# An S5 state-space step inside a streaming encoder: 32-wide TensorE tiles, three slabs in each step, tokens in natural order

## The reference, cut to what matters

```
z = h @ w_in;  u, q, k, v, g_s, g_a = split(z)
# 64 groups of 16 channels, 64 complex states each
bu[l] = Bbar[g] @ u[l, g]                      # 16 channels -> 64 complex states
s[l]  = Abar * s[l-1] + bu[l]                  # over the tokens (prompt from 0, sample from the given state)
y[l]  = Re(C[g] @ s[l]);  y = gelu(y + ssm_d * u);  y = y * sigmoid(y @ w_glu)
```

## Time and profile before

| | us |
|---|---|
| median of 3 runs | 1407.69 |
| lowest, highest | 1404.42, 1412.64 |
| the profiled execution | 1413.75 |
| its span | 1411.8 |
| mean granted TensorE clock in it | 0.946 of full speed |

### The profile page before, as it was taken

One profiled execution on the slowest core, in us unless ns is written; L12 is line 12 of the kernel. 1 busy time (PEld: TensorE's weight loads), 2 busy tenths in 40 slices (PEclk: granted clock), 3 DMA queues, 4 the chain that ended last, 5 costly groups with the idle time before them and its releaser, 6 DMA issues.

```text
span 1411.8 us, 22570 instructions
## 1 busy us (share of the span) xinstructions
PE 1279.8 (91%) x9314; PEld 1247.9 (88%) x9314; DVE 717.4 (51%) x1022; ACT 529.5 (38%) x960; POOL 309.6 (22%) x276
## 2 busy tenths in 40 slices
PE   3999899996849899999987989988999999999996
PEld 3999888996748799999987988988999999999995
DVE  5344888888786543454466333235432433433433
ACT  6446434443325562333544223224312312312322
POOL 1069988888100000000211000024000000000020
PEclk9999999998768989999999999888999999999996
DMA  6142112221100053332344420220232232332311
GB/s 177 58 146 65 56 49 90 94 94 47 40 14 1 7 186 109 107 115 76 113 157 131 146 60 1 60 61 24 81 99 65 81 100 60 90 88 70 94 30 67
DMA packets 183410, 113.29 MB, mean 80 GB/s; under 512 B 6976, under 2 KB 175872, under 8 KB 183008
## 3 DMA queue, kind: packets, MB, share of 16 engines
q1 hardware_dynamic: 178400, 104.56, 24.9%
q10 hardware_dynamic: 4928, 7.56, 1.5%
HBM read 100.11 MB, written 12.12 MB: 79 GB/s over the span
## 4 chain that ended last, share of the span: by engine, by line
PE 72%; DVE 16%; ACT 6%; issue 4%; DMA 2%; POOL 0%; SPq 0%; DVEq 0%; ACTq 0%; POOLq 0%
PE gp L1546 29%; PE gp L1923 29%; DVE z L1283 3%; ACT ub L757 3%; PE sp L1784 2%; PE sp L1898 2%; DVE wL L1044 1%; PE gp L1875 1%; DVE rot L1262 1%; PE sp L1664 1%; PE gp L1683 1%; PE sp L1652 1%; DVE rot L1264 1%; DVE x L1123 1%; DVE raw L1103 1%
## 5 line engine op out<-in xcount | busy, mean ns | idle before, releaser
L1044 DVE TENSOR_TENSOR wL<-wraw,wH 128x1024 fp32r<-128x1024 f32 x164 | 216.3, 1319 | 138.5 <-ACT wH L615 138.1
L615 ACT ACTIVATE wH<-wraw 128x1024 fp32r<-128x1024 f32 x164 | 172.8, 1054 | 241.0 <-PE gp L1923 121.4
L1546 PE MATMUL gp<-aH,wH 128*128 128x288 f32 (+1 forms) x1088 | 241.9, 305 | 10.9 <-DVE aL L1079 4.0
L590 POOL TENSOR_TENSOR acc<-acc,sq 128x576 f32<-128x576 f32 x28 | 41.8, 1492 | 924.8 <-ACT sq L667 924.8
L1546 PE MATMUL gp<-aL,wH 128*128 128x288 f32 (+1 forms) x1088 | 237.8, 301 | 0.0
L1546 PE MATMUL gp<-aH,wL 128*128 128x288 f32 (+1 forms) x1088 | 237.6, 301 | 0.0
L1546 PEld LDWEIGHTS gp<-aH,wH 128*128 128x128 f32 x1088 | 181.4, 195 | 13.6 <-issue 11.8
L1546 PEld LDWEIGHTS gp<-aL,wH 128*128 128x128 f32 x1088 | 181.3, 194 | 0.0
L1546 PEld LDWEIGHTS gp<-aH,wL 128*128 128x128 f32 x1088 | 180.8, 194 | 0.0
L1923 PE MATMUL gp<-aH,wH 128*128 128x288 f32 x512 | 112.0, 301 | 9.1 <-DVE aL L1110 4.5
L1923 PE MATMUL gp<-aH,wL 128*128 128x288 f32 x512 | 110.8, 298 | 0.0
(11 more groups left out here) (298 smaller groups left out, 2215.4 us busy)
## 6 DMA issues: line engine op xcount, KB each, us to landing
wraw<-in_w_ff SPq DMA_DIRECT2D x64, 512.0 KB, 4.1
wraw<-in_w_in SPq DMA_DIRECT2D x36, 512.0 KB, 3.8
gates_scratch<-sq ACTq DMA_DIRECT2D x16, 288.0 KB, 2.2
gate<-gates_scratch SPq DMA_DIRECT2D x16, 288.0 KB, 4.5
wraw<-in_p_att SPq DMA_DIRECT2D x8, 512.0 KB, 4.3
wraw<-in_w_glu SPq DMA_DIRECT2D x8, 512.0 KB, 4.3
wraw<-in_p_ssm SPq DMA_DIRECT2D x8, 512.0 KB, 4.2
wraw<-in_w_out SPq DMA_DIRECT2D x8, 512.0 KB, 4.2
```

The lines of the kernel that those rows point to most:

```text
L590: g.tensor_tensor(acc[:], acc[:], sq[:, k % 2], ALU.add).then_inc(sq_used, 1)
L615: s_.activation(wH[s][:], wraw[w][:], ACT.Copy).then_inc(wh_done, 1)
L1044: v.tensor_tensor(wL[s][:], wraw[w][:], wH[s][:], ALU.subtract).then_inc(wl_done, 1)
L1546: last = mm(gp[:, b + h, 0:n], w[:, k, :], y[:, k, c0:c0 + n], start=(k == 0 and w is wH[s] and y is xh), stop=(k == KT - 1 and w is wL[s]))
```

## The change

- `SSM_SLABS` has three slabs for each of eight steps (12 to 35). TensorE's step m is now: slab, outputs(m-1), slab, table(m+1), slab, inputs(m+1); outputs(7) stays in the tail.
- ub and `u_build` are gone. TensorE reads u from z directly, with a step of four tokens (`by_time`), and writes y into PSUM with one bank for each of the four tokens of a block.
- `table`: the Toeplitz table is built as four column tiles of 32, with 64 columns each; toep shrinks to 128x128, and ScalarE copies it, in one operation.
- `inputs`: 32 matmuls on row tiles of 32 rows (pair j on rows 32j, PSUM bank j), four accumulated for each.
- `outputs`: 32 matmuls on column tiles of 32 and 40 on 32x32 tiles at (32j, 32j).
- `y_out` is one operation of 128x576 and sits inside `scan_and_turn` of the next step.
- `e_table` keeps one multiplication on GpSimd; er comes from a third sine on ScalarE, rho from four scaled copies on ScalarE, and the factor 2 of ei moves into VectorE's operations. zm gets a third buffer.
- ScalarE's copy of the final states and the eight stores move behind `soften(0)`; the transposes for it move behind band_scores(1) and y_out(7), and band_step(0) waits for the copy.

```diff
-SSM_SLABS = {m: list(range(12 + 4 * m, 16 + 4 * m)) for m in range(-1, 5)}
-SSM_SLABS[5], SSM_SLABS[6] = [32, 33], [34, 35]
+SSM_SLABS = {m: list(range(12 + 3 * m, 15 + 3 * m)) for m in range(8)}
...
+        Y0, T0 = 2 * NB, 3 * NB
+        v_slot = [sp_[:, :, c * NB:(c + 1) * NB] for c in range(2)]
+        y_slot = sp_[:, :, Y0:Y0 + NB]
+
+        def by_time(ap):
+            return ap.rearrange("p (c s) -> p s c", s=SB)
...
-                if m >= 2:
-                    pool.wait_ge(y_ps, m - 1)
-                zb = zm[m % 2]
+                if m >= 3:
+                    pool.wait_ge(y_ps, m - 2)
+                zb = zm[m % 3]
...
-                g.tensor_tensor(eim[:], e0, e1, ALU.mult)
-                seq(g.tensor_tensor(erm[:], e0, e0, ALU.mult))
-                g.tensor_scalar(eim[:], eim[:], 2.0, 0.0, ALU.mult, ALU.add)
-                g.tensor_scalar(erm[:], erm[:], -2.0, 1.0, ALU.mult, ALU.add)
-                g.tensor_tensor(rho[m % 2][:], bk(thl[:, 2, ds(PB * m, PB)], [P, PB, NB]),
-                                cmask[:].unsqueeze(1).broadcast_to([P, PB, NB]), ALU.mult).then_inc(e_ready, 1)
+                g.tensor_tensor(ei[m % 2][:], e0, e1, ALU.mult).then_inc(e_ready, 1)
...
+                if m >= 2:
+                    act.wait_ge(h_ready, m - 1)
+                for j in range(PB):
+                    s_.activation(rho[m % 2][:, j, :], cmask[:], ACT.Copy, scale=thl[:, 2, PB * m + j:PB * m + j + 1])
                 seq(s_.activation(earg[:, 1], earg[:, 0], ACT.Abs))
+                s_.activation(er[m % 2][:].rearrange("p j c -> p (j c)"), earg[:, 1], ACT.Sin, scale=-TWO_PI, bias=halfpi[:, 0:1])
...
-                for j in range(PB):
-                    src = z[32 * j:32 * j + 32, ds(m, 1), :].rearrange("p o (c s) -> p (o s) c", s=SB)
-                    for s in range(SB):
-                        last = s_.activation(ub[b][32 * s:32 * s + 32, j, :], src[:, s], ACT.Copy)
-                last.then_inc(u_built, 1)
...
+                if m >= 2:
+                    act.wait_ge(y_ps, m - 1)
+                s_.activation(toep[m % 2][:].rearrange("p (b c) -> p b c", b=2), sp_[:, 0:2, T0:T0 + 64], ACT.Copy).then_inc(toep_cp, 1)
...
             def y_out(m):
                 dve.wait_ge(y_ps, m + 1)
-                for j in range(PB):
-                    r = slice(32 * j, 32 * j + 32)
-                    zu = z[r, ds(m, 1), :].rearrange("p o (c s) -> p (o s) c", s=SB)
-                    for s in range(SB):
-                        last = v.scalar_tensor_tensor(zu[:, s], zu[:, s], gains[r, ds(8 * G_D + m, 1)],
-                                                      sp_[32 * s:32 * s + 32, j // 2, (j % 2) * NB:(j % 2 + 1) * NB],
-                                                      ALU.mult, ALU.add)
-                last.then_inc(y_evac, 1)
+                u = by_time(z[:, m, :])
+                v.scalar_tensor_tensor(u, u, gains[:, 8 * G_D + m:8 * G_D + m + 1], y_slot, ALU.mult, ALU.add).then_inc(y_evac, 1)
...
+            def ssm_step(m):
+
+                t0 = SSM_SLABS[m][0] + AHEAD
+                turn_in(m)
+                split_l(t0, t0)
+                scan_and_turn(m)
+                split_l(t0 + 1, t0 + 1)
+                split_l(t0 + 2, t0 + 2)
...
+                    pe.wait_ge(v_read, m)
+                    pe.wait_ge(toep_cp, m)
+                    pe.wait_ge(y_evac, m)
...
+                for h in range(2):
                     for c in range(2):
-                        last = mm(sp_[0:32, 2, j * P:(j + 1) * P], xm[:, c, j, SB - 1, :],
-                                  zm[b][:, c, j, 0:SB, :].rearrange("p s k -> p (s k)"), start=(c == 0), stop=(c == 1))
+                        for j in range(PB):
+                            last = mm(sp_[32 * j:32 * j + 32, h, T0:T0 + 64], xm[:, c, SB - 1, j, :],
+                                      zm[m % 3][:, c, j, 2 * h:2 * h + 2, :].rearrange("p s k -> p (s k)"),
+                                      start=(c == 0), stop=(c == 1), tile_position=(0, 32 * j))
...
+                for c in range(2):
+                    for q in range(SB):
+                        for j in range(PB):
+                            r = slice(32 * j, 32 * j + 32)
+                            last = mm(sp_[:, j, c * NB:(c + 1) * NB], xt[r, c, q, :], by_time(z[r, m, :])[:, q],
+                                      start=(q == 0), stop=(q == SB - 1), tile_position=(32 * j, 0))
                 last.then_inc(v_ps, 1)
...
+                for q in range(SB):
+                    for c in range(2):
+                        for j in range(PB):
+                            mm(y(q, j), zm[m % 3][:, c, j, q + 1, :], hs[:, c, j, 0:NB], start=(c == 0), stop=False,
+                               tile_position=(0, 32 * j))
+                for q in range(SB):
+                    for n in range(q + 1):
+                        for j in range(PB):
+                            r = slice(32 * j, 32 * j + 32)
+                            last = mm(y(q, j), toep[m % 2][r, 32 * n:32 * n + 32], by_time(z[r, m, :])[:, q - n],
+                                      start=False, stop=(n == q), tile_position=(32 * j, 32 * j))
                 last.then_inc(y_ps, 1)
...
+                a, b, c = SSM_SLABS[m]
+                z_slab(a, a)
+                if m:
+                    outputs(m - 1)
+                z_slab(b, b)
+                if m < 7:
+                    table(m + 1)
+                z_slab(c, c)
+                if m < 7:
+                    inputs(m + 1)
```

More of the change, by code:

```diff
@@ L167, in build @@
         hs = nxt("hs", [P, 2, PB, NB + 1])
[L168 removed]
+        er, ei = ([nxt(f"{n}0", [P, PB, NB])] for n in ("er", "ei"))
         assert off[0] <= S0 + 52700, off[0] - S0
@@ L705, in evac_z @@
                     last.then_inc(evac_act, 1)
+                elif t < 8:
+                    s_.activation(halves(z[:, t, :]), result(j), ACT.Copy).then_inc(evac_act, 1)
                 else:
@@ L1309, in _ @@
-            with dve.Fori(0, 2) as i:
-                seq.enter(i, 0, 2 * 7)
-                for b in range(2):
-                    m = 2 * i + b
-                    ssm_step(m, b, [12 + 4 * m + j for j in range(4)])
-            seq.leave(2)
-            for m in range(4, 7):
-                ssm_step(m, m % 2, SSM_SLABS[m])
-            turn_in(7, 1)
-            scan_and_turn(7, 1)
+            for m in range(8):
+                ssm_step(m)
             dve.wait_ge(dist_ready, 1)
@@ L1625, in _, with table @@
                         last.then_inc(xt_ps, 1)
-            def table(m, b, first=False):
+            def table(m):
                 pe.wait_ge(tab_ready, m + 1)
-                if first:
+                if m == 0:
                     pe.wait_ge(xt_cp, 10)
@@ L1670, in _ @@
             z_slab(9, 1)
-            table(0, 0, first=True)
+            table(0)
             z_slab(10, 2)
             z_slab(11, 3)
-            inputs(0, 0)
+            inputs(0)
             def band_scores(n, b, c0, keys):
@@ L1692, in sample_keys, with ssm_step @@
                 return (ks if kv % 2 == par else ksx)[:, kv // 2, :]
-            def ssm_step(m, b, slabs):
-                half = len(slabs) // 2
-                j0 = slabs[0] if isinstance(slabs[0], int) else 0
-                for j in range(half):
-                    z_slab(slabs[j], j0 + j)
-                table(m + 1, 1 - b)
-                z_slab(slabs[half], j0 + half)
-                outputs(m, b)
-                if half == 2:
-                    z_slab(slabs[3], 3)
-                inputs(m + 1, 1 - b)
-            for m in range(7):
-                ssm_step(m, m % 2, SSM_SLABS[m])
+            def ssm_step(m):
+                a, b, c = SSM_SLABS[m]
+                z_slab(a, a)
+                if m:
+                    outputs(m - 1)
[3 more added lines that the diff above has]
+                z_slab(c, c)
+                if m < 7:
+                    inputs(m + 1)
+            for m in range(8):
+                ssm_step(m)
             pe.wait_ge(evac_act, T_PATT)
@@ L1729, in _ @@
             band_scores(0, 0, 128, k_keys(0, 128))
-            outputs(7, 1, last_one=True)
-            for w in range(2):
-                for c in range(2):
-                    last = tr(sp_[0:PAIRS, 3, (2 * w + c) * P:(2 * w + c + 1) * P], fin[:, c, :, w], ident[:])
-            last.then_inc(va_ps, 1)
+            outputs(7)
             def turn_out(n, b):
@@ L1796, in _ @@
             pe.wait_ge(y_evac, 9)
+            for w in range(2):
+                for c in range(2):
+                    last = tr(sp_[0:PAIRS, w, c * P:(c + 1) * P], fin[:, c, :, w], ident[:])
+            last.then_inc(va_ps, 1)
+            pe.wait_ge(va_cp, 7)
             band_step(0, 0, False, True, None, v_one(0), lambda: band_scores(2, 0, 0, k_keys(2, 0)))
```

159 lines of the change are left out of this document (63 added, 96 removed).

## The result

The changed kernel takes 1400.24 us (median of 10 runs, 1394.36 to 1403.31), the kernel before 1406.80 (10 runs on the same chips, 1403.79 to 1413.00). The ratio is 0.9944 with a 95% interval of 0.9921 to 0.9966: faster by 0.6%, some 8 us, where 42 were forecast. The profiled execution has a span of 1398.2 us, against 1411.8 before. The forecast of 1366 and its own range (1352 to 1388) are missed; the wide range up to 1413 holds the result, but only because it covered the cases without a gain.

What follows compares the result with a forecast made beforehand. TensorE, busy 91% of the span, was taken as the bound, with exposed waits for VectorE. Loop -35.4 and tail -7 gave -42 us: 1371.4, or 1366 from the runs' median; own range 1352 to 1388, 8-in-10 range to 1413.

Steps and rivals of the forecast that it cites:

- The waits go: SSM loop: TensorE's waits ahead of output matmuls (14.1 us) and input matmuls (19.0 us) fall to near zero.
- Four tiles at once: TensorE's small passes on 32-wide tiles: four run together, 0.031 us a pass of 144 columns; chance 0.53.
- two at a time: Rival, chance 0.15: small TensorE passes come no faster than 0.056 to 0.062 us, limited by instruction issue; 1413 us.
- one by one: Rival, chance 0.13: in outputs, the four diagonal 32x32 tiles writing one PSUM bank take turns; 1426 us.
- no overlap: Rival, chance 0.03: TensorE's small tiles do not run side by side; 29.7 us a step, 1514 us.
- the borders: Entries into and exits from tiled groups on TensorE: eight a step at 0.15 us each, 1.2 us.
- I take no cost: TensorE's small passes reading z every four elements pay nothing extra: braw's 0.88 ns an element gives 0.126 us a pass.
- stride: Rival, chance 0.04: each strided TensorE pass costs 0.30 us instead of 0.123, 45 us in all; 1411 us.
- just fits: SSM loop: GpSimd's work, 27.7 us a step at most, stays within TensorE's step of 28.9 us.
- the GpSimd rival: Chance 0.12: GpSimd, slowed by a denser VectorE, sets the step at 31 us, giving 14 us back; 1380 us.
- The tail: From the SSM loop's end to the last operation of score(1): 29.7 us falls to 23, 7 less.
- I cost it nothing: Eight state stores moved ahead of the second softmax delay it 2 to 3 us; no cost, 3 without cover.

Runs made afterwards that it cites:

- e2: The changed kernel with inputs and the Toeplitz part reading 144 neighbouring elements instead of every fourth (wrong tokens): 1373.4 us, ratio 0.9749.
- e3: The changed kernel reading every second element in inputs and every third in the Toeplitz part (wrong tokens): 1382.90 us, one execution.
- e1: The kernel before, unedited, executed once more for its profile: 1396.76 us.
- e5: The changed kernel with ScalarE writing the first eight slabs reordered, so TensorE's small passes read neighbours with the right tokens: 1373.57 us, ratio 0.9761.

## Why the prediction was right and wrong

**The waits go: right.** Both exposed waits are gone and the clock is 1.00 through the loop.

**Four tiles at once: right**, from two tiles in the earlier trace rows. Column, row and diagonal tiles all average 0.034 a pass or less when they read neighbours; the rivals *two at a time*, *one by one* and *no overlap* fall. The Trainium skill's rule in TensorEngine Tiling (Array Packing), Restrictions and Gotchas, against row tiles in one bank, does not show here for diagonal tiles that write different partitions of the bank: no loss in e2. The terms: table 1.46 (forecast 1.93), inputs 2.17 (1.97), outputs 4.68 (4.43); a slab is 6.58 rather than 6.45, and the borders, forecast at 1.2, are in that and cost 0.4 at most. The step was forecast at 28.9 and is 28.1 without stride and GpSimd.

**"For TensorE the nearest row is the load of braw with a step of 16 elements ... I take no cost": this is the step that failed.** It costs 0.13 us in each of 36 rounds, 4.7 us a step, 33 in seven steps, and 5 more in inputs(0) and outputs(7). The rival named *stride* priced it at 0.18 and gave it a chance of 0.04. Its mechanism was the right one, and of the 11 us by which its time (1411) was too high 7 are its price. The row that the step rested on could not carry it. The same trace holds the contiguous twin of these loads, with the same shapes (32 rows, 128 columns, and passes that stream 32 columns):

```profile
39.67 0.38 PEld L1599 LDWEIGHTS sp<-ident,st 32*128 32x128 f32 x5 [0.16 <-issue]
```

One of these loads takes 137 ns in the mean and the next starts 0.06 us later. Of the 32 loads with a step of 16 elements one takes 198 ns, and they follow each other every 0.11 us. So the row did not show that a stride is hidden: it showed a pace nearly halved by it, to 0.88 ns an element, and this pace happens to equal that of a float32 pass of 144 columns. The prediction read the strided row without its twin. And it was a load, while the change strides the moving operand, whose reading sets a round in e2 and e3. ScalarE's and VectorE's rows, where the operation does wait for its own read, had shown the cost as well, and they were set aside.

**GpSimd "just fits" against 28.9: wrong, but hidden.** It needs 25.3 us in the changed kernel's step, where it waits for TensorE, but 28.4 in the shorter step of e2 with its denser VectorE (forecast 27.7), and with this work the step stays at 29.7 to 29.9. With a free stride the forecast would still have missed by a microsecond a step: e2 gave 1373, near the 1380 of the GpSimd rival.

**VectorE** was forecast at 25.6 at most and has 23.4; its output step at 1.3 and has 1.28. Right.

**The tail** was forecast at -7, from 29.7 us to 23, up to the last operation of score(1). It is 23.8 now, -5.9 (and -5.4 up to the first transposes). The scores began 9.3 us after the last slab (forecast 9.4), outputs(7) took 8.3 (8.9). The terms were close; the prediction's sum of them was not: 9.4 + 8.9 + 1.5 + 4.5 are 24.3, not 23. Missed was the wait of 1.4 us for the state stores, "I cost it nothing": that cover, scores(2) and the first mix, was a little too short. It lies behind these marks, in the stretch that came out at +0.1.

**Not seen at all: +5.5 us in the feed-forward loop.** The working priced instructions on TensorE's queue, not the fetching of them. The change touches nothing there, yet TensorE now waits for its own instructions at three points. Of the 5.5, 4.3 are more idle time (7.0 us against 2.7).

In sum: -35.4 forecast in the loop, -7.7 came, the difference being the strides (33 in the loop) less the 5 or so by which the other terms were better; tail -5.4 for -7; +5.5 unforeseen. That leaves -7.6, and the medians differ by 6.6 to 8. The agreement is in part luck: the execution profiled before took 1413.75, more than each of the ten runs, and against e1, the fastest (1396.76), the loop gave 3.1 us and not 7.7. What doesn't hang on the execution before is the distance to the forecast: the loop takes 249.0 us where 221.3 were forecast, inputs(0) 2.1 more, and the feed-forward loop 5 to 7 more.

## What to carry to other kernels

Price a strided read by an instruction that is itself paced by that read, on the same operand; before a row is taken to say that a stride is free, look for its contiguous twin of the same shape in the same trace. Where an operand is read many times over, reorder it once on an engine with time to spare: here eight strided copies of 1.2 us on ScalarE take away 38 us of TensorE's time, of which e5 gets 27 and the rest needs a shorter GpSimd. When one bound is lifted, size the next by its rows under contention, not by its rows today: GpSimd's work grew from 25.3 to 28.4 us, and one of its operations doubled, as the step got shorter.

## What the runs showed of the hardware that was not expected

- Four tiles of 32 read their float32 moving operand at full rate with a step of one element, at over 0.9 of it with two, at 0.66 with three, at half with four.
- A weight load of 32 rows and 128 float32 columns takes 137 ns and follows the last one after 0.06 us when it reads neighbours, 198 ns and 0.11 us with a step of 16 elements.
- TensorE idled 5.5 us at three points of a loop in which it had not idled before, with 30 instruction packets more (91 instead of 61) in a program that executes 11% more instructions elsewhere; so did five more profiles of such programs, and in four with the loop written out there was none of it. Whether the length or the place of the code decides was not tried.
- At a granted clock of 1.00 the same 2972 to 2976 matmuls took 392.7 us in one execution and 399.8 in another. The records have no cause for it.
- Of two GpSimd roundings of 1.60 and 1.52 us (e2; 0.67 and 1.52 in the changed kernel), merged into one instruction with two additions, 3.07 remained.
